# The first expert's rows selected in turned form by products with the one-hot columns, and its weight places refilled in quarters

## The reference, cut to what matters

```python
def one_group(hs):
    logits = jnp.einsum('ld,de->le', hs, w_router, preferred_element_type=jnp.float32)
    aff = jax.nn.softmax(logits, axis=-1)
    g, idx = lax.top_k(aff.T, cap)
    xg = hs[idx]
    a = jnp.einsum('ecd,edf->ecf', xg, w_gate)
    u = jnp.einsum('ecd,edf->ecf', xg, w_up)
    y = jnp.einsum('ecf,efd->ecd', jax.nn.silu(a) * u, w_down)
    y = y * g[..., None].astype(y.dtype)
    out = jnp.zeros((L, D), y.dtype).at[idx.reshape(-1)].add(y.reshape(-1, D))
    return out.astype(hs.dtype)
```

## Time and profile before

| | |
|---|---|
| median of 3 runs | 1719.86 us |
| the profiled execution | 1718.28 us |
| its span in the profile | 1716.7 us |
| TensorE busy | 1611.5 us, 94% |
| VectorE, ScalarE busy | 725.8 us (42%), 458.9 us (27%) |
| granted TensorE clock, mean | 0.982 of 2.4 GHz |
| bytes moved | 577.90 MB, mean 337 GB/s |

### The profile page before, as it was taken

The page is one execution under the profiler, slowest core; times in us unless marked ns, Lnnn a source line. Parts: engine busy times, 40 slices in busy tenths (PEclk is TensorE's granted clock), DMA queues, the critical chain, the costliest instruction groups (busy, mean ns, idle before and its releaser), DMA issues.

```text
span 1716.7 us, 22475 instructions
## 1 busy us (share of the span) xinstructions
PE 1611.5 (94%) x9448; PEld 979.3 (57%) x9448; DVE 725.8 (42%) x1402; ACT 458.9 (27%) x805; POOL 33.8 (2%) x39
## 2 busy tenths in 40 slices
PE   7999999999999999999999988979888898888898
PEld 5787999998999999787222322323223223223332
DVE  3778889878886558684111110101101111101101
ACT  3426633448654435543000000000000000000001
POOL 0101000000000001100100000000000000000000
PEclk9999999999999999999999999999999999999999
DMA  9865489891466463248999999999999999999997
GB/s 389 350 246 214 170 319 345 322 355 67 188 255 226 168 224 144 99 154 357 397 428 430 430 431 431 430 430 431 431 430 431 430 432 429 432 431 429 431 431 300
DMA packets 46323, 577.90 MB, mean 337 GB/s; under 512 B 5232, under 2 KB 6288, under 8 KB 10256
## 3 DMA queue, kind: packets, MB, share of 16 engines
q1 hardware_dynamic: 46224, 576.47, 81.7%
HBM read 575.40 MB, written 1.05 MB: 336 GB/s over the span
## 4 chain that ended last, share of the span: by engine, by line
PE 63%; DMA 32%; DVE 2%; ACT 1%; SPq 1%; issue 1%; DVEq 0%; ACTq 0%
DMA RING_T<-in_w_up 30%; PE P L1389 15%; PE P L975 4%; PE P L977 4%; PE P L976 4%; PE P L573 4%; PE P L1416 3%; PE P L993 2%; PE P L992 2%; PE P L994 2%; PE P L582 2%; DMA RING_T<-in_ada_w 1%; DMA RING_T<-in_w_down 1%; PE P L1163 1%; PE P L1165 1%; PE P L1164 1%
## 5 line engine op out<-in xcount | busy, mean ns | idle before, releaser
L1389 PE MATMUL P<-RING_T,SCR 128*34 128x512 f32 x928 | 433.9, 623 | 86.6 <-DMA RING_T<-in_w_up 86.6
L1390 PE MATMUL P<-RING_T,SCR 128*34 128x512 f32 x960 | 449.1, 623 | 0.0
L1389 PEld LDWEIGHTS P<-RING_T,SCR 128*34 128x34 f32 x928 | 103.6, 116 | 363.1 <-issue 362.4
L3001 DVE TENSOR_TENSOR SCR<-P,SCR 34x512 f32<-34x512 f32 x64 | 44.4, 693 | 542.7 <-ACT SCR L2113 542.7
L1416 PE MATMUL P<-RING_T,SCR 128*34 128x512 f32 x480 | 217.1, 595 | 0.9 <-DMA RING_T<-in_w_down 0.9
L1417 PE MATMUL P<-RING_T,SCR 128*34 128x512 f32 x480 | 217.1, 595 | 0.0
L2113 ACT ACTIVATE SCR<-P 34x512 f32<-34x512 f32 x64 | 37.7, 589 | 570.4 <-PE P L1390 570.4
L975 PE MATMUL P<-SCF 128*128 128x256 f32 x640 | 181.1, 283 | 0.0
L977 PE MATMUL P<-SCF 128*128 128x256 f32 x640 | 181.1, 283 | 0.0
L976 PE MATMUL P<-SCF 128*128 128x256 f32 x640 | 181.1, 283 | 0.0
L975 PEld LDWEIGHTS P<-SCF 128*128 128x128 f32 x640 | 122.9, 192 | 0.0
(11 more groups left out here) (452 smaller groups left out, 2514.8 us busy)
## 6 DMA issues: line engine op xcount, KB each, us to landing
RING_T<-in_w_up SPq DMA_DIRECT2D x58, 2048.0 KB, 21.5
RING_T<-in_w_down SPq DMA_DIRECT2D x57, 2048.0 KB, 19.9
RING_T<-in_w_gate SPq DMA_DIRECT2D x56, 2048.0 KB, 18.4
RING_T<-in_ada_w SPq DMA_DIRECT2D x24, 2048.0 KB, 10.1
RING_T<-in_ffn_w SPq DMA_DIRECT2D x22, 2048.0 KB, 8.3
RING_T<-in_ffn_w SPq DMA_DIRECT2D x22, 1024.0 KB, 7.0
RING_T<-in_ab_w_in SPq DMA_DIRECT2D x7, 2048.0 KB, 13.9
RING_T<-in_w_in SPq DMA_DIRECT2D x6, 2048.0 KB, 8.6
```

Source lines behind the costliest of these rows:

```text
L1389: pe.matmul(u.t[0:CAP, :], xs, wg.v(KC, 512)[:, c, :], start=c == 0, stop=c == KC - 1)
L1390: ins = pe.matmul(u.t[64:64 + CAP, :], xs, wu.v(KC, 512)[:, c, :], start=c == 0, stop=c == KC - 1)
```

## The change

- `first_picks(pair)` takes the place of `pick(0)` and `turn_picks(0)`. It multiplies with exchanged roles: a 128-column piece of `FT` is the stationary operand and the 34 one-hot columns move, so that the result comes out turned, 128 x 34 for each of the 8 chunks of the width. No copy and no transpose follow, only VectorE's product with the gain (`gather_first`), two chunks a time. Chunks 0 to 3 are selected ahead of the first gate product; chunks 4 and 5 between the third and the fourth gate chunk, chunks 6 and 7 between the fifth and the sixth.
- VectorE makes the other experts' one-hot columns between `gather_first(1)` and `gather_first(2)`. Three `pe_busy` calls go.
- `pick(e + 1)` moves ahead of `down(e, 1)`, for every expert.
- `REFILLS` extends the cut transfers from four tiles to twelve: all that take a place which expert 0 leaves, and two which the first gate and up tiles of expert 1 leave. They are quarters (1024 columns, 4 KB in a partition), except for the first four pieces of the first pair, which are eighths (512 columns; before, the first two pieces).

Before, these were six whole tiles, L3295 with 128x4096 each. The whole diff:

```diff
--- before.py
+++ after.py
@@ -94,10 +94,12 @@
 LOADS += ["q2", "k2", "v2", "cx", "cc", "cb", ("o2", 0), ("o2", 1)]
 LOADS += [(x, 0, i) for i in range(3) for x in "gu"] + [("d", 0, 0)]
 
-QUARTERS = [("d", 0, 0), ("g", 1, 0), ("u", 1, 0), ("g", 1, 1)]
-
-PIECES = [(0, 1, 2, 4, 6, 8), (0, 2, 4, 6, 8)]
-PIECES_OF = {x: len(PIECES[n // 2]) - 1 for n, x in enumerate(QUARTERS)}
+REFILLS = [([("d", 0, 0), ("g", 1, 0)], ("g", 0, 0)), ([("u", 1, 0), ("g", 1, 1)], ("g", 0, 1)),
+           ([("u", 1, 1), ("g", 1, 2)], ("g", 0, 2)), ([("u", 1, 2)], ("d", 0, 0)), ([("g", 1, 3)], ("d", 0, 1)),
+           ([("u", 1, 3)], ("d", 0, 2)), ([("d", 1, 0)], ("d", 0, 3)), ([("d", 1, 1), ("d", 1, 2)], ("g", 1, 0))]
+PIECES = {x: (0, 2, 4, 6, 8) for _, x in REFILLS}
+PIECES["g", 0, 0] = (0, 1, 2, 3, 4, 6, 8)
+PIECES_OF = {y: len(PIECES[x]) - 1 for tiles, x in REFILLS for y in tiles}
 
 BESIDE = {("g", 1, 3): 3, ("u", 1, 3): 2, ("d", 1, 0): 4}
 BESIDE.update({("g", 2, 1): 3, ("u", 2, 1): 2, ("g", 2, 2): 4, ("g", 3, 0): 3, ("u", 3, 0): 2, ("g", 3, 1): 4})
@@ -370,7 +372,7 @@
         self.first = {x: Slot(t, self.sem[f"ex{i}"], 16, None) for i, (x, t) in enumerate(zip(keys, places))}
         there = [self.first[x] for x in keys]
         for x, i in BESIDE.items():
-            there[i] = self.first[x] = Slot(places[i], self.sem[f"ex{i}"], there[i].n + 16, there[i])
+            there[i] = self.first[x] = Slot(places[i], self.sem[f"ex{i}"], there[i].n + 16 * PIECES_OF.get(x, 1), there[i])
 
     def cc(self, name, a=0, b=None):
         if name in LOFF:
@@ -1342,10 +1344,8 @@
     def pick(e):
 
         u = pe_bank(nc, k, ("picks", e), takers=2)
-        if e == 0:
-            pe_busy(nc, k, u, 1)
         for i, (r, m) in enumerate(TILES):
-            pe.wait_ge(s["onehot"], i + 1 + 3 * min(e, 1))
+            pe.wait_ge(s["onehot"], i + 4)
             for half in range(2):
                 ins = pe.matmul(u.t[64 * half:64 * half + CAP, :], v.OH[0:m, i, e * CAP:(e + 1) * CAP],
                                 v.FT[0:m, i, half * 512:half * 512 + 512], start=i == 0, stop=i == 2)
@@ -1357,11 +1357,23 @@
         for half in range(2):
             u, r = pe_bank(nc, k, ("turned", e, half)), 64 * half
             if half == 0:
-                pe_busy(nc, k, u, 2 if e == 0 else 0)
                 pe.wait_ge(t.taken, t.done)
             for c in range(4):
                 ins = pe.transpose(u.v(4, CAP)[:, c, :], v.XT[r:r + CAP, c * 128:(c + 1) * 128], ident[r:r + CAP, r:r + CAP])
             ins.then_inc(u.full, 1)
+
+    def first_picks(pair):
+        u = pe_bank(nc, k, ("first", pair))
+        if pair == 0:
+            pe_busy(nc, k, u, 1)
+        for a in range(2):
+            c = 2 * pair + a
+            for i, (r, m) in enumerate(TILES):
+                if c == 0:
+                    pe.wait_ge(s["onehot"], i + 1)
+                ins = pe.matmul(u.v(2, CAP)[:, a, :], v.FT[0:m, i, c * 128:(c + 1) * 128], v.OH[0:m, i, 0:CAP],
+                                start=i == 0, stop=i == 2)
+        ins.then_inc(u.full, 1)
 
     def back_map(g):
         u = pe_bank(nc, k, ("back", g))
@@ -1377,18 +1389,22 @@
         pieces = (e, i) == (E_N - 1, 3)
         if not pieces:
             pe.wait_ge(wu.sem, wu.n)
-        if (e, i) == (0, 0):
-            pe_busy(nc, k, u, 1)
         for c in range(KC):
+            if (e, i) == (0, 0):
+                if c in (3, 5):
+                    first_picks((c + 1) // 2)
+                if c % 2 == 0:
+                    t = P["first", c // 2]
+                    pe.wait_ge(t.taken, t.done)
             if pieces and c % 4 == 0:
                 pe.wait_ge(s[f"lastu{c // 4}"], 16)
-            if i == 0 and c % 4 == 0:
+            if e and i == 0 and c % 4 == 0:
                 t = P["turned", e, c // 4]
                 pe.wait_ge(t.taken, t.done)
             xs = k.tokens_of(e, c)
             pe.matmul(u.t[0:CAP, :], xs, wg.v(KC, 512)[:, c, :], start=c == 0, stop=c == KC - 1)
             ins = pe.matmul(u.t[64:64 + CAP, :], xs, wu.v(KC, 512)[:, c, :], start=c == 0, stop=c == KC - 1)
-            if e == 0 and i < 2 and c + 1 in PIECES[i][1:-1]:
+            if c + 1 in PIECES.get(("g", e, i), ())[1:-1]:
                 ins.then_inc(s["first_used"], 1)
         ins.then_inc(u.full, 1)
         wg.left = wu.left = (u.full, u.n)
@@ -1415,6 +1431,8 @@
             first, end = i == 0 and c == 0, i == 3 and c == 3
             pe.matmul(u.t[0:CAP, :], hs, w.v(4, 1024)[:, c, 0:512], start=first, stop=end)
             ins = pe.matmul(u.t[64:64 + CAP, :], hs, w.v(4, 1024)[:, c, 512:1024], start=first, stop=end)
+            if e == 0 and c < 3:
+                ins.then_inc(s["first_used"], 1)
         if i < 3:
             ins.then_inc(s["edown"], 1)
             w.left = (s["edown"], 3 * e + i + 1)
@@ -1450,8 +1468,8 @@
                 pe.matmul(u.t[:, :], v.OGT[0:NP, 7, M + 128 * i:M + 128 * i + 128], v.Y[0:NP, 1, half * 512:half * 512 + 512],
                           start=False, stop=True, skip_group_check=True).then_inc(u.full, 1)
 
-    pick(0)
-    turn_picks(0)
+    first_picks(0)
+    first_picks(1)
     for e in range(E_N):
         gate_up(e, 0)
         if 1 <= e <= 8:
@@ -1466,10 +1484,10 @@
         u = pe_bank(nc, k, ("eo", e), takers=2, hold=True)
         down(e, 0, u)
         turn_hidden(e, 3)
+        if e < E_N - 1:
+            pick(e + 1)
         for i in range(1, 4):
             down(e, i, u)
-            if i == 1 and e < E_N - 1:
-                pick(e + 1)
             if i == 2 and e < E_N - 1:
                 turn_picks(e + 1)
         P.drop(("eo", e))
@@ -2121,8 +2138,9 @@
         for i in range(1, 4):
             gate(e, i)
         if e < E_N - 1:
-            t = P["turned", e, 1]
-            act.wait_ge(t.full, t.n)
+            if e:
+                t = P["turned", e, 1]
+                act.wait_ge(t.full, t.n)
             pick(e + 1)
         else:
             act_table(nc, SET_EXP)
@@ -2975,7 +2993,7 @@
             dve.tensor_tensor(v.XG[:, e % 2, 4 * half:4 * half + 4, :], u.v(4, CAP), weighed_by(4, half, CAP),
                               ALU.mult).then_inc(u.taken, 1)
 
-    for a, b in ((0, 1), (1, E_N)):
+    def one_hot(a, b):
         for i, (r, m) in enumerate(TILES):
             if a == 0:
                 dve.scalar_tensor_tensor(out=v.SV[0:m, i, :], in0=u.v(3, 16)[0:m, i, :], scalar=1.0, in1=v.MSK[0:m, i, :],
@@ -2988,9 +3006,19 @@
             io = k.cc("iota")[0:m, :].rearrange("p (a s) -> p a s", a=1).to_broadcast([m, b - a, CAP])
             sv = v.SV[0:m, i, a:b].rearrange("p (e a) -> p e a", a=1).to_broadcast([m, b - a, CAP])
             dve.tensor_tensor(o, io, sv, ALU.is_equal).then_inc(s["onehot"], 1)
-    pick(0)
+
+    def gather_first(pair):
+        u = P["first", pair]
+        dve.wait_ge(u.full, u.n)
+        dve.tensor_tensor(v.XG[:, 0, 2 * pair:2 * pair + 2, :], u.v(2, CAP), weighed_by(2, pair, CAP), ALU.mult).then_inc(u.taken, 1)
+
+    one_hot(0, 1)
     dve.wait_ge(s["routed"], 2)
-    gather_picks(0)
+    gather_first(0)
+    gather_first(1)
+    one_hot(1, E_N)
+    gather_first(2)
+    gather_first(3)
 
     def hidden(e, i):
         u, n = P["egu", e, i], 4 * e + i
@@ -3277,17 +3305,18 @@
     beside(4, (u.full, u.n))
 
     used = 0
-    for i, tiles in enumerate((QUARTERS[0:2], QUARTERS[2:4])):
-        for a, b in zip(PIECES[i], PIECES[i][1:]):
+    for tiles, left in REFILLS:
+        for a, b in zip(PIECES[left], PIECES[left][1:]):
             used += b < KC
-            for x, e, j in tiles:
-                w = k.ring[x, e, j]
+            for x, e, i in tiles:
+                w = k.weight_at(x, e, i)
                 if b < KC:
                     sp.wait_ge(s["first_used"], used)
                 else:
                     sp.wait_ge(*w.prev.left)
                 o, p = SLOT // KC * a, SLOT // KC * b
-                sp.dma_start(w.t[:, o:p], A[names[x]][e, j][:, o:p]).then_inc(w.sem, 16)
+                sp.dma_start(w.t[:, o:p], A[names[x]][e, i][:, o:p]).then_inc(w.sem, 16)
+
     def beside_ring(x, e, i):
 
         w = k.weight_at(x, e, i)
@@ -3298,7 +3327,7 @@
         if e:
             for i in range(4):
                 for x in "gu":
-                    if (x, e, i) not in QUARTERS and (x, e, i) != ("u", E_N - 1, 3):
+                    if (x, e, i) not in PIECES_OF and (x, e, i) != ("u", E_N - 1, 3):
                         beside_ring(x, e, i)
         if e == 5:
 
@@ -3313,7 +3342,7 @@
                 a, b = 2 * D * c, 2 * D * (c + 1)
                 sp.dma_start(w.t[:, a:b], A["w_up_2"][e, 3][:, a:b]).then_inc(s[f"lastu{c}"], 16)
         for i in range(4):
-            if e and (e < E_N - 1 or i < 2):
+            if e and (e < E_N - 1 or i < 2) and ("d", e, i) not in PIECES_OF:
                 beside_ring("d", e, i)
     for i, n, first in ((2, 2, 0), (3, 4, 2)):
         w = k.ring["d", E_N - 1, i]
```

## The result

The change makes the kernel slower. Its median is 1723.45 us (19 runs, 1721.61 to 1725.16), against 1719.77 us for the kernel before in the same series (19 runs, 1718.14 to 1721.17): a ratio of 1.002 with the interval 1.0014 to 1.0026, that is 3.7 us. The profiled execution took 1723.66 us, its span is 1722.3 us.

What follows compares the result with a forecast made beforehand. Expert stage bound by bytes delivered before the even 430 GB/s. Terms 2.2 - 0.3 - 0.65 - 0.7 + 1.45 - 0.45 gave a 1.5 us gain: 1716.8 profiled, median 1718.3 with the 1.58 offset; range 1715.6 to 1721.0.

Steps and rivals of the forecast that it cites:

- What bounds the kernel: Expert stage: bound by bytes at an even 430 GB/s; what counts is bytes delivered when that rate begins.
- the price of a selection pass: Ahead of the first gate product: 24 passes at 0.105 us, 2.5 us, so that product starts 2.2 us earlier.
- the upper bound of 0.123: Selection passes: highest price per pass considered, in us, from L1311, 16 passes in 1.97 us with 128 moving columns.
- The pieces: Refills of the first pair's places: first issued at 809.0 instead of 811.24, last at 817.6, 0.35 us later than before.
- Just dry, 0.1 us: Transfer queue before the fifth piece's data at 817.1: the first four pieces, 2.10 MB, run out for 0.1 us.
- lead at 824: Bytes delivered by 824 us ahead of the kernel before: 1.9 us, 0.82 MB.
- Quarters: Eight more cut tiles: 4 KB rows flow at 417 GB/s, not 445, in 834 to 844, costing 0.65 us.
- the slow rival: Quarters flow at 364 GB/s in themselves, making the kernel 4.8 us slower, 1724.6; chance 0.10.
- The dry places: Thin transfer stretches from 844 to 865 us: filled by quarters, worth 1.45 us.
- The moved selection: Next expert's selection ahead of the second down tile: delays the `TAIL` refill, queue dry for 0.7 us before 848.5.
- that ceiling: Until 848.5 us at most seven tiles are released, 14.68 MB, which caps what can be delivered.
- The lead is spent: Rival: dry place before `TAIL`, small pieces at the start or dearer selections leave no gain, 1719.6 to 1719.9; chance 0.16.

Runs made afterwards that it cites:

- the kernel with the clock kept: The changed kernel with two idle products ahead of each of the first two pairs of selections, instead of one ahead of the first: 1722.86 us, 1.0023 of before.
- the kernel with two token tiles: The changed kernel with those added idle products, expert 0's selection leaving out the third token tile (last 16 tokens): 1718.28 us, 0.9992 of before.
- the kernel with all pairs ahead: The changed kernel with all four pairs of turned selections ahead of the first gate product, none between gate chunks: 1726.93 us, 1.0036 of before.

## Why the prediction was wrong

It said 1718.3 us and a range up to 1721.0; the kernel takes 1723.45. The profiled span, before and after, shows more than the medians: it was forecast as 1715.2 us and is 1722.3, 7.1 us more, where the median is 5.2 us more. The 1.58 us by which the median of before lay above its profiled execution were added to the forecast and did not come back (the kernel after has 1723.66 profiled and 1723.45 in the median), so that the forecast's number looks about 2 us better than its account, by luck.

- **What bounds the kernel: right.** The even stretch, the waits for up tiles (13.3 us in 1000 to 1100 us, 14.3 before) and the end are as they were, and the spans follow the bytes delivered at 873 us.
- **The step that failed is the price of a selection pass.** "I take 0.105: 2.5 us" rested on L1336, 12 passes in 1.13 us, as the nearest row. That mean hides two kinds. The weight loads of the kernel before by form show it, and could have been read (line, operation, tiles, shapes, count; busy us and mean ns):

```profile
L1336 PEld LDWEIGHTS P<-SCR,C 128*128 128x128 f32 x6 | 0.7, 190 | 0.2 <-DVE SCR L2958 0.2
L1336 PEld LDWEIGHTS P<-SCR,C 128*16 128x16 f32 x4 | 0.2, 94 | 0.0
L1350 PEld LDWEIGHTS P<-SCR 128*34 128x34 f32 x8 | 0.4, 111 | 1.0 <-DVE SCR L2990 0.6 <-issue 0.3
```

  Half of L1336's twelve passes load 16 columns, in 94 ns, the other half 128 columns in 190. The turned form loads 128 columns in every pass, for the tile of 16 tokens too, to move 34; the old form loaded 34 columns, twelve times, to move 512. In the kernel after, the same view has:

```profile
L1374 PEld LDWEIGHTS P<-SCR 128*128 128x128 f32 x32 | 4.9, 217 | 2.4 <-issue 1.9 <-DVE SCR L3008 0.3
L1374 PEld LDWEIGHTS P<-SCR 16*128 16x128 f32 x16 | 2.8, 214 | 0.4
```

  Loads fill 7.7 of the 8.7 us that the 48 passes take. At the full clock a pass costs 0.147 to 0.156 us in the mean, above the upper bound of 0.123.

  The rows of these loads overlap (190 ns each at the full clock, and 0.11 us apart), so the price itself is read from the starts of the single passes in the traces. In L1336 of the kernel before, the passes that load 128 columns start 0.11 us apart, those that load 16 mostly 0.025. In the kernel with the clock kept, the passes on one token tile start 0.11 us apart too, though they move 34 columns and not 16. But where the selection goes from a tile of 128 tokens to the tile of 16, or back, the next pass starts only after 0.20 to 0.21 us and the one behind it after 0.13. That makes 0.12 us for each change, three times in twelve passes of the turned form, since it goes through all three token tiles for every chunk; in the kernel with two token tiles the starts stay 0.11 us apart. The old form changes once in its twelve passes (L1350: 0.52 us instead of 0.42). So 0.105 was nearly right for a pass that follows one of its own kind, and the changes of tile height have no term in the sum.

  The Trainium skill says of the loads themselves (TensorE: Matmul & The Clock Gate, "LDWEIGHTS (loading the stationary operand)"): their time goes by the columns and not by the rows, and the trace agrees, 214 ns for 16 rows and 217 for 128 (182 and 190 with the clock kept).
- **A second step failed: the clock was not in the sum at all.** Idle products were counted as removed, and the granted clock of 1.00 in the earlier trace rows as given. From about 807.1 to 814 it was 0.50 (0.79 in 806 to 808, 0.50 in 808 to 812, 0.92 in 812 to 824). In this trace that cost 1.2 us in the train (4.93 against 24 x 0.156) and 2.1 us in the first three gate chunks (809.93 to 814.62, 4.7, against 3 x 0.86). The kernel with the clock kept shows what of these 3.3 us can be had: its last piece goes out 1.9 us earlier, and the idle products that hold the clock up cost the other 1.4.
- **The pieces, "issued at 809.0, 809.9, 810.8, 812.9, 815.9 and 817.6": wrong by these two.** They went out at 811.90, 813.61, 814.74, 817.51, 821.15 and 822.87. For the last one, 2.0 us come from the start of the first gate product, 2.1 from the chunks at half clock, and 2 x (1.8 - 1.26) = 1.1 from the pairs between (814.62 to 816.42 and 818.26 to 820.06). By cause, the price of the passes makes 2.3 us of this (1.2 in the train, 1.1 in the pairs) and the clock 3.3, while the train began 0.2 us sooner than forecast and lacked the 0.1 us for the one-hot tiles. In this trace the clock is thus the larger part: by the forecast's own sum, and if no more of the queue ran dry, 2.3 us alone would give 1720.6 us, still within its range. "Just dry, 0.1 us" became a queue that delivers 12 GB/s at 821, and the "lead at 824" of 0.82 MB a lag of 1.4 MB (12 x 119 KB).
- **Quarters: right in the mechanism, in size low.** 417 GB/s was taken for 834 to 844 and 418 to 420 measured; the slow rival (364) fell. The dry places were filled, with 2.4 us gained by the refills alone. The account of the profiled executions explains 0.9 us of that (24.5 less 24.1 MB); the rest is that the profiled execution of before, from which the sum started, was itself 1.5 us below its median, and that such an offset does not carry over (after: 1723.66 profiled, 1723.45 in the median).
- **The moved selection: its size is near what was taken, but not for the reason given.** 0.7 us was taken for a queue that is dry at 848.5 us because all of 14.68 MB have been delivered. The kernel never came near that ceiling: counted from 812 us it had 12.1 MB by 848.3, and 844 to 848.3 ran at 420 GB/s. What shows comes behind it, 391 GB/s in 848.3 to 861 where the refills alone have 418, which is 0.8 us. The 0.7 us between the medians of the refills with and without the move lie within the noise.
- **The rivals.** "The lead is spent" named 0.123 us a pass as its worst case, where nothing is left. It had the place right and stopped short: the loss of the turned form, 0.32%, is 5.5 us (4.5 between the medians), the refills return 2.4, and what is left, 3.1 us (2.1), agrees with the 3.7 measured as far as the intervals tell. The rival nearest in number, 1724.6 us, put the loss down to slow quarters; they ran at 418 to 420 GB/s, so its number was luck.

What stays open: how the loss of the turned form divides between the price of a pass and the clock in the medians, since no kernel kept the clock without paying for it; and what TensorE does in the 0.12 us of a change between a tile of 128 tokens and one of 16. No run kept the tile of 16 and took all its passes together, so what such an order would return was not measured.

## What to carry to other kernels

When the operands of a product change roles, price the pass by its weight load as well as by the columns that move: read the loads by shape, don't take a mean over rows that mix widths, and count how often the new order changes from a tall tile to a short one. Ask what the granted clock will be when a stretch is replaced by many short products. And where a queue of transfers is released piece by piece by an engine, each microsecond put between two pieces counts for what it lets run dry, while cutting the transfers finer behind it is a gain that can be had alone.

## What was not expected of the hardware

- **TensorE's clock falls while its row shows it busy.** In the kernel after, PE is busy for 2.00 of 2.00 us in 806 to 808, and the granted clock falls in that window, while it works through passes that load 128 columns and move 34; it comes back during the gate products that follow. In the kernel with all pairs ahead it falls in 808 to 809 and stays at 0.50 until 821. In the kernel with the turned form alone the same 24 passes run through at 1.00, and it falls behind them (0.55 in 809 to 810); why earlier in one and later in the other, no run shows. With two idle products of 256 columns ahead of each of the first two twelves it stays at 1.00, and so it does with the one-hot columns as the loaded side, where 256 or 512 columns move. The Trainium skill (TensorE: Matmul & The Clock Gate, "What's actually happening") has the clock follow how busy the array has been; the busy time of this profile does not tell that, as the rows show.
- **Passes that load 128 columns and move few start 0.11 us apart, and a change of tile height adds 0.12.** Whether 16 columns move (L1336) or 34 (L1374), the distance at the full clock is 0.11 us, and 0.21 in the kernel after while the clock is at 0.50; a change from 128 rows to 16 or back adds 0.12. In 819 to 820 the kernel after shows weight loads for 0.92 of 1.00 us, at the full clock and with the matmul row at 1.00. Moving 34 columns instead of 512 saved nothing: 48 passes at 0.156 are 7.5 us, the twelve of the old form 2.89.
- **Quarters of 0.5 MB ran at 418 to 420 GB/s** from 824 to 873 in the kernel with the refills alone, against 430 for whole tiles behind them; beyond this difference the 26 more transfers had no price that could be seen.
